# A two-block hybrid network in one launch: the first attention regrouped, the conformer stage fed further ahead

## The reference

```python
# first attention: 8 "full" heads (8 previous chunks, i.e. all keys so far, with a learned relative
# bias) and 8 heads in a window of 2 previous chunks (linear bias, sinks, 2 key/value heads)
qa, ka, va, qb, kb, vb = jnp.split(h @ w_in, cuts, axis=-1)
qa = rmsnorm(heads(qa, H_A), q_norm_a); ka = rmsnorm(heads(ka, H_A), k_norm_a)
oa = band_attention(qa, ka, heads(va, H_A), A_PREV_CHUNKS, bias_a, None)
qb = rmsnorm(heads(qb, H_B), q_norm_b); kb = rmsnorm(heads(kb, H_B_KV), k_norm_b)
ob = band_attention(qb, kb, heads(vb, H_B_KV), B_PREV_CHUNKS, bias_b, sinks)
return jnp.concatenate([oa, ob], axis=-1) @ w_out
# each head of q and k: y = x * rsqrt(mean(x*x over its 64 channels) + eps) * gain

# conformer convolution (second block)
a, gate = jnp.split(h @ w_pw1 + b_pw1, 2, axis=-1)
u = a * sigmoid(gate)
u = depthwise_conv_31_taps(u) + b_dw
u = silu(layer_norm(u, ln_g, ln_b))
return u @ w_pw2 + b_pw2
```

## Time and profile before

| | us |
|---|---|
| median of the runs (3 runs) | 3264.16 |
| the profiled execution | 3262.22 |
| its span, first to last instruction | 3260.4 |
| mean granted TensorE clock | 0.977 |
| PE busy in the span | 3083.4 (95%) |
| DVE, ACT, POOL busy | 1521.9, 1307.6, 1186.2 |
| first attention, from its first projection to its output projection | 13.4 to 290.0 |
| conformer, from its first projection to the end of the last mean matmul | 1608.4 to 1816.4 |

### The profile page before, as it was taken

One profiled execution on the slowest core, in us unless ns is written; L12 is line 12 of the kernel. 1 busy time (PEld: TensorE's weight loads), 2 busy tenths in 40 slices (PEclk: granted clock), 3 DMA queues, 4 the chain that ended last, 5 costly groups with the idle time before them and its releaser, 6 DMA issues.

```text
span 3260.4 us, 40032 instructions
## 1 busy us (share of the span) xinstructions
PE 3083.4 (95%) x13814; PEld 2393.4 (73%) x13814; DVE 1521.9 (47%) x2127; ACT 1307.6 (40%) x2069; POOL 1186.2 (36%) x511
## 2 busy tenths in 40 slices
PE   6898999998998899999988999999989999899998
PEld 4566788876675578888755777888867787788886
DVE  5542555336616735552278633333147763333222
ACT  4663444323334534443322534443233343344432
POOL 3121444442342034444432532444432253244443
PEclk8998999999998899999999999999999999999999
DMA  4121322332220022223311321222321132122332
GB/s 151 40 77 33 93 94 92 101 97 77 77 90 1 1 84 91 92 95 99 101 47 44 123 78 58 91 96 91 103 83 59 59 116 85 43 93 91 95 97 90
DMA packets 74459, 263.18 MB, mean 81 GB/s; under 512 B 8664, under 2 KB 8928, under 8 KB 74096
## 3 DMA queue, kind: packets, MB, share of 16 engines
q1 hardware_dynamic: 68400, 249.07, 24.5%
q10 hardware_dynamic: 3648, 7.46, 0.6%
q0 software_dynamic: 2304, 5.24, 0.6%
HBM read 259.59 MB, written 2.15 MB: 80 GB/s over the span
## 4 chain that ended last, share of the span: by engine, by line
PE 43%; issue 33%; POOL 14%; DVE 7%; ACT 2%; POOLq 0%; DMA 0%; ACTq 0%; DVEq 0%; SPq 0%
POOL w_lo L547 14%; PE bank L610 11%; PE bank L612 11%; PE bank L611 11%; PE bank L1109 2%; DVE bank L1785 2%; DVE bank L1877 1%; PE bank L1236 1%; PE bank L1239 1%; PE bank L1057 1%; PE bank L1058 0%; PE bank L1059 0%; PE bank L686 0%; PE bank L726 0%; PE bank L1253 0%
## 5 line engine op out<-in xcount | busy, mean ns | idle before, releaser
L547 POOL TENSOR_TENSOR w_lo<-w_raw,w_hi 128x1024 fp32r<-128x1024 f32 x475 | 1144.8, 2413 | 1901.5 <-ACT w_hi L2049 1901.5
L2049 ACT ACTIVATE w_hi<-w_raw 128x1024 fp32r<-128x1024 f32 x475 | 501.1, 1056 | 668.7 <-DMA w_raw<-w_glu_out 157.0
L610 PE MATMUL bank<-xh,w_hi 128*128 128x512 f32 x1864 | 745.3, 400 | 18.9 <-POOL w_lo L547 14.2
L611 PE MATMUL bank<-xl,w_hi 128*128 128x512 f32 x1864 | 740.0, 397 | 0.0
L612 PE MATMUL bank<-xh,w_lo 128*128 128x512 f32 x1864 | 739.8, 397 | 0.0
L610 PEld LDWEIGHTS bank<-xh,w_hi 128*128 128x128 f32 x1864 | 351.7, 189 | 114.9 <-POOL w_lo L547 21.6
L611 PEld LDWEIGHTS bank<-xl,w_hi 128*128 128x128 f32 x1864 | 351.8, 189 | 86.1 <-issue 1.7
L612 PEld LDWEIGHTS bank<-xh,w_lo 128*128 128x128 f32 x1864 | 351.8, 189 | 85.8
L1341 DVE TENSOR_TENSOR xt<-bank,xt 128x512 f32 x72 | 49.8, 692 | 504.1 <-PE bank L612 504.1
L612 PE MATMUL bank<-hh,w_lo 128*128 128x512 f32 x704 | 279.1, 396 | 0.0
L610 PE MATMUL bank<-hh,w_hi 128*128 128x512 f32 x704 | 279.1, 396 | 0.0
(11 more groups left out here) (341 smaller groups left out, 4659.2 us busy)
## 6 DMA issues: line engine op xcount, KB each, us to landing
w_raw<-w_ffn_in SPq DMA_DIRECT2D x88, 512.0 KB, 3.5
w_raw<-w_glu_in SPq DMA_DIRECT2D x88, 512.0 KB, 3.5
w_raw<-w_ffn_out SPq DMA_DIRECT2D x48, 512.0 KB, 3.5
w_raw<-w_glu_out SPq DMA_DIRECT2D x48, 512.0 KB, 3.5
w_raw<-w_ssm_in SPq DMA_DIRECT2D x41, 512.0 KB, 3.5
w_raw<-w_pw SPq DMA_DIRECT2D x24, 512.0 KB, 3.5
w_raw<-w_diff_in SPq DMA_DIRECT2D x24, 512.0 KB, 3.5
w_raw<-w_attn_in SPq DMA_DIRECT2D x18, 512.0 KB, 3.6
```

What stands on the lines that cost most here:

```text
L547: pool.tensor_tensor(w_lo[:, slot, :], w_raw[:, slot, :], w_hi[:, slot, :].bitcast(F32), ALU.subtract).then_inc(w_split, 1)
L610: pe.matmul(b, wh, hi[:, k, 0:n], start=(k == 0), stop=False)
L611: pe.matmul(b, wh, lo[:, k, 0:n], start=False, stop=False)
L2049: act.activation(w_hi[:, slot, :], w_raw[:, slot, :], ACT.Copy).then_inc(w_half, 1)
```

## The change

In the first attention: the chunk order becomes kb, qb pair 0, vb, the other qb, then (qa, ka, va) by pair. The sums of squares of a group of chunks go as rows into one bank of 32 rows (`pick`, a 128 by 32 selection); there are four groups; the root and the reciprocal (in two halves) are taken once per group on 32 rows, and a second matmul (`heads`, 32 by 128) spreads a chunk's rows to bank 5, from which DVE scales. All q, k and v of the full heads have a place of their own. The windowed heads use one set of banks only, with turn in the same step and outputs one step later; the full heads alternate between two sets as before. More units are fed per step (11 per 4 places), so that the projections end in step 12. The 128 by 128 outputs of a pair are kept until its four tiles are there, and then transposed, stored and split together. `b_pt` now lies on the memory input `m_in`, whose load moves from the kernel's start to the first ffn. In the conformer: 7 taps on PE and 24 on DVE, four buffers `c_u`, the gate stays in its PSUM bank, the projections run one pair further ahead, and ACT takes one more slab before it copies `m_hi`. The core of the diff:

```diff
-        CPE = 8
+        CPE = 7
-        VALUES = (1, 8, 11, 14, 17)
+        VALUES = (2, 8, 11, 14, 17)
+        GROUPS = ((0, 1), (3, 4, 5), (6, 7, 9, 10), (12, 13, 15, 16))
+        EARLY = (8, 8, 8, 4, 4, 4, 4)
+        SLOT0 = len(EARLY)
         def attn_fed(x):
-            return min(18 * KD, 34 + 9 * (x + 1) // 6) if x >= 0 else 34
+            if x < SLOT0:
+                return sum(EARLY[:x + 1])
+            return min(18 * KD, sum(EARLY) + 11 * (x - SLOT0 + 1) // 4)
+        def attn_events():
+            sums = {attn_at(c) + 1: c for c in NORMED}
+            roots = {attn_at(g[-1]) + 1: n for n, g in enumerate(GROUPS)}
+            shared = [(attn_at(c) + 1, c) for c in VALUES]
+            for x, n in roots.items():
+                shared += [(x + 3 + (i if n else 0), c) for i, c in enumerate(GROUPS[n])]
         def step_bank(m, half):
-            return bank[2 + 2 * (m % 2) + half]
+            return bank[2 + half + (2 if is_rel(m) and m % 2 == 0 else 0)]
+        def turn_step(m):
+            return m + 1 if is_rel(m) else m
+        def output_step(m):
+            return m + 2 if is_rel(m) else m + 1
# PE, first attention
-                    pe.matmul(bank[7][:], head_ones[:], sq[:, 0, :], start=True, stop=True).then_inc(q_sum, 1)
+                def total(c):
+                    pe.wait_ge(q_sq, n + 1)
+                    if i == 0 and g:
+                        pe.wait_ge(q_root, g)
+                    pe.matmul(bank[4][0:32, :], pick[:, 30 - 2 * i:62 - 2 * i], sq[:, 0, :], start=(i == 0),
+                              stop=(c == GROUPS[g][-1]), skip_group_check=True).then_inc(q_sum, 1)
+                def share(k):
+                    if k:
+                        pe.wait_ge(*released(k))
...
+                    pe.wait_ge(q_rec, 2 * g + 2)
+                    pe.matmul(bank[5][:], heads[:, i * P:(i + 1) * P], acc[0:32, :], start=True, stop=True).then_inc(q_bc, 1)
                 def score(m):
-                    if m >= 2:
-                        pe.wait_ge(b_copied, 2 * (m - 1))
+                    elif m == NB4 + 1:
+                        pe.wait_ge(b_copied, 2 * NB4)
+                    elif m:
+                        pe.wait_ge(b_copied, 2 * (m - 1) if is_rel(m) else 2 * m)
                 def outputs(m):
-                        pe.wait_ge(b_ol, m)
+                        pe.wait_ge(b_otok, m)
-                def turn_out(m):
-                    pe.wait_ge(b_otok, m + 1)
-                    pe.transpose(bank[6][:, P:2 * P], b_tok[:, m % 2, :], ident[:]).then_inc(b_ot, 1)
+                def turn_out(pair):
+                    pe.wait_ge(b_otok, NT * (pair + 1))
+                    if pair:
+                        pe.wait_ge(b_ol, pair)
+                    for t in range(NT):
+                        mm = pe.transpose(bank[7][:, t * P:(t + 1) * P], b_tok[:, t, :], ident[:])
+                    mm.then_inc(b_ot, 1)
# DVE, first attention
-                    dve.reciprocal(bank[7][:], bank[7][:]).then_inc(q_rec, 1)
+                def inverse(g, part):
+                    dve.wait_ge(q_root, g + 1)
+                    r = acc[0:32, part * 256:(part + 1) * 256]
+                    dve.reciprocal(r, r).then_inc(q_rec, 1)
# PE, conformer
-                project(1)
-                for p in range(KD):
-                    if p < KD - 1:
-                        project(2 * p + 2)
-                    else:
-                        feed(KD)
+                for c in range(1, 3):
+                    project(c)
+                conv(0)
+                for c in range(3, 6):
+                    project(c)
+                for p in range(1, KD):
                     conv(p)
                     if p >= 3:
                         mean(p - 3)
-                    if p < KD - 1:
-                        project(2 * p + 3)
+                    if p < KD - 2:
+                        project(2 * p + 4)
+                        project(2 * p + 5)
+                    elif p == KD - 2:
+                        feed(KD)
# DVE, conformer
-                    dve.tensor_tensor(c_g[:, p % 2, :], bank[(b0 + 1) % BANKS][:], rstd[:], ALU.mult).then_inc(bank_free, 1)
+                    dve.tensor_tensor(g[:], g[:], rstd[:], ALU.mult).then_inc(c_gate, 1)
-                    dve.scalar_tensor_tensor(c_u[:, p % 3, CONVW - 1:], c_a[:, p % 2, :], col("pw1_b", 2 * p),
-                                             c_g[:, p % 2, :], ALU.add, ALU.mult).then_inc(c_new, 1)
+                    dve.scalar_tensor_tensor(c_u[:, p % 4, CONVW - 1:], c_a[:, p % 2, :], col("pw1_b", 2 * p),
+                                             bank[(st.chunk0 + 2 * p + 1) % BANKS][:], ALU.add, ALU.mult).then_inc(bank_free, 1)
-                        if p < KD - 1 and n == (5 if p else 7):
-                            gated(p + 1)
-                        if p < KD - 1 and n == (7 if p else 9):
-                            entered(p + 1)
+                        if p == 0 and n == 2:
+                            gated(1)
+                        if p == 0 and n == 4:
+                            entered(1)
+                        if p < KD - 2 and n == 8:
+                            gated(p + 2)
+                        if p < KD - 2 and n == 9:
+                            entered(p + 2)
# ACT, conformer
                 next_slab()
                 gate(0)
                 next_slab()
+                next_slab()
                 act.wait_ge(m_landed, 16)
                 act.activation(m_hi[:], m_in[:], ACT.Copy).then_inc(m_half, 1)
                 diag(1)
+                gate(1)
+                next_slab()
                 for p in range(KD - 1):
-                    next_slab()
-                    gate(p + 1)
-                    next_slab()
-                    if p + 2 < KD:
+                    if p < KD - 2:
+                        next_slab()
+                        gate(p + 2)
+                        next_slab()
                         diag(p + 2)
# constants and the memory input
-                dve.tensor_copy(head_ones[:], cst[:, 3 * P:4 * P]).then_inc(cst_ready, 1)
+                dve.tensor_copy(pick[:], cst[:, 3 * P:3 * P + 64]).then_inc(cst_ready, 1)
+                dve.tensor_copy(heads[:].rearrange("p (a n) -> p a n", n=64),
+                                ident[0:32, 0:8].unsqueeze(2).broadcast_to([32, 8, 64])).then_inc(cst_ready, 1)
-            act.dma_start(m_in[:], A["memt"]).then_inc(m_landed, 16)
+                if s == "ffn0":
+                    act.dma_start(m_in[:], A["memt"]).then_inc(m_landed, 16)
```

More of the change, by code:

```diff
@@ L381, in attn_at @@
+        def attn_at(c):
             x = 0
-            while attn_fed(x) < min(KD * (c + 1) + extra, 18 * KD):
+            while attn_fed(x) < KD * (c + 1):
                 x += 1
-            return x + (1 if KD * (c + 1) + extra > 18 * KD else 0)
-        def step_bank(m, half):
-            return bank[2 + 2 * (m % 2) + half]
-        VALUES = (1, 8, 11, 14, 17)
-        NORMED = [c for c in range(18) if c not in VALUES]
-        UNITS = {}
+            return x
+        def attn_events():
[4 more added lines that the diff above has]
+                shared += [(x + 3 + (i if n else 0), c) for i, c in enumerate(GROUPS[n])]
+            return sums, roots, sorted(shared)
@@ L1925, in attn @@
                     for f in range(3):
[L1926 to L1936 removed]
+                        events(SLOT0 + 3 * m + f)
+                        if f == 0 and m < BM:
+                            weigh(m)
+                        for j in range(NT - 1, BM, NT):
+                            if f == 2 and output_step(j) == m:
+                                low(j // NT)
                 vt[0] += 5
@@ L2428, in square, with rooted, value, events @@
                     act.activation(sq[:, 0, :], norm_slot(c), ACT.Square).then_inc(q_sq, 1)
[L2430 to L2439 removed]
+                def rooted(g):
+                    act.wait_ge(q_sum, sum(len(chunks) for chunks in GROUPS[:g + 1]))
+                    if g:
+                        act.wait_ge(q_bc, sum(len(chunks) for chunks in GROUPS[:g]))
+                    act.activation(acc[0:32, :], bank[4][0:32, :], ACT.Sqrt, scale=1.0 / 64, bias=eps[0:32, 0:1])\
+                        .then_inc(q_root, 1)
+                def value(c):
+                    act.wait_ge(v_turned, VALUES.index(c) + 1)
+                    act.activation(b_v[:, value_slot(c), :], bank[5][:], ACT.Copy).then_inc(v_ready, 1)
+                def events(x):
+                    for c in NORMED:
+                        if attn_at(c) == x:
+                            square(c)
+                    if x in ROOTS:
+                        rooted(ROOTS[x])
+                    for at, c in SHARED:
+                        if at == x and c in VALUES:
+                            value(c)
+                    while turned[0] < 18 + LEAD and attn_fed(x) >= min(KD * (turned[0] - LEAD) + 6, 18 * KD):
+                        next_slab()
```

285 lines of the change are left out of this document (126 added, 159 removed).

## The result

The changed kernel takes 3286.8 us (median of 4 runs, 3282.2 to 3291.3) against 3265.2 in the same job: ratio 1.0074, 95% interval 1.0061 to 1.0086. I had forecast 3252, range 3232 to 3270. The profiled execution took 3282.2 (span 3280.3), 20.0 more than before's 3262.2.

The account below looks back on a forecast made before the run. PE and issue hold three quarters of the chain of waits, with engines waiting in turn. From 3262.2, 5 us lost in the attention and 17 won in the conformer give 3250, or 3252 against the median; range 3232 to 3270.

Parts of the forecast that it names:

- The conformer: Conformer stage: PE and DVE work side by side, pairs take 18 us instead of 22.2; 17 us won.
- its stop: Conformer start: PE stands 7.4 us before project(3), because the later `m_hi` copy delays POOL's `memory_lower` and subtractions.
- PE as bound of steps 0 to 12: First attention: with 104 projection units and the added norm matmuls, PE limits these steps, 118 us in total.
- the price of the added matmuls: First attention: separate norm sums and spreadings, 0.86 us each; the extra 13 cost PE 11.2 us.
- rival C: Windowed attention steps: scores wait for copies from the single bank set; 1.5 us a step gives 3276; chance 0.15.
- X + 133.0: Conformer: end of the last tap, 1797.9, counted from X = 1664.9, after the opening stop, three chunks and conv(1).
- Steps 16 to 31, without projections: Late first attention: priced from earlier projection-free steps at 82.3 us, bounds 73.3 and 91; step 31 starts at 278.3.
- rival B: First attention: clock stays down from step 14; steps 16 to 31 take 91 instead of 82, total 3261; chance 0.18.
- To step 0: First attention: step 0 starts at about 60.8 instead of 58.3, with 40 units done instead of 34.
- Steps 0 to 12: First attention: PE does 104 units plus attention and norm matmuls; step 12 starts at 173.
- Steps 12 to 15: First attention: last group's norm and bare chains take 25 us; step 16 starts at 198, effectively 196.
- The end: First attention, score 31 to output projection: two waits for `low` go, 16.4 us instead of 17.9.

Follow-up runs that it names:

- keep3: The changed kernel plus 108 extra bf16 matmuls with unused results in attention steps 16 to 33: 3263.0 us, ratio 1.0001.
- slow_feed_clock: slow_feed with the extra unused matmuls of keep3, begun in step 15: 3256.2 us, ratio 0.9976 to the kernel before.
- pool_order: keep13 with POOL's second bias table loads after the output projection's first three subtractions instead of before them: 3258.6 us, ratio 0.9976 to the kernel before.
- keep13: keep3 with the extra matmuls begun in step 13 instead of 16: 3262.6 us.
- slow_feed: The changed kernel feeding 12 projection units per five places instead of 11 per four, so projections end in step 14: 3269.6 us, ratio 1.0017.
- cheap_norm: keep13 with 9 norm sums and 9 spreadings cut to 128 of 512 columns, output not the reference's: 3245.0 us, ratio 0.993 to the kernel before.
- before_short_recip: The kernel before with DVE's 13 head norm reciprocals over 128 of 512 columns, values not the reference's: 3246.0 us, ratio 0.995.
- best_clock: m_hi_early plus the extra unused matmuls of keep3 in steps 26 to 33 of the first attention: 3235.9 us, ratio 0.9916 to the kernel before.
- m_hi_early: conf_only with the copy `m_hi` one slab earlier, in its place before the change: 3241.7 us, ratio 0.9936 to the kernel before.
- conf_only: The kernel before with only the conformer part of the change: 3246.1 us, ratio 0.995.

## Why the prediction was wrong

**Right.** The conformer: 17 forecast, 18 measured, with its stop (7.4 and 7.41) and the pairs 17.7 apart, DVE going from one to the next without a wait. PE as bound of steps 0 to 12 and the price of the added matmuls (11.2 for 13; doubling them costs 13.7). The windowed steps on one set of banks: among their scores only that of step 15 waited for `b_pt`, 0.47 us, so rival C, my slower case, named the wrong mechanism.

**Right by luck.** `entered` at 0.74: I gave it 0.7 because its operand would come from PSUM. What the traces of both kernels show is another cause, told in the last section. There are also slips in the working that move nothing: steps 0 to 15 of before feed 72 units, not 73; a pair took 22.8 us, not 22.2; and the sum to X + 133.0 has four rounds of 17.7 in it, where the text says five.

**The step that failed** is "Steps 16 to 31, without projections": 82.3 us (80.3 from step 16's own start, 198 to 278.3), upper bound 91; measured 105.1. I took its price from four steps that ran at a mean clock of 0.85 and put the upper bound for four at "about 25", 2.5 more, which is about the 2.7 that I had worked out for one of the four, step 27 (its score, bias matmuls and transposes). Four such steps took 29.2 to 30.3 here (steps 19 to 30). The rows above show why: everything that PE does in the loop is longer in every step, the outputs too, and ACT's copies and the next score wait for them. That bound was no bound. The mechanism was rival B's, at 0.18 and priced +14 with that same bound; keep3 shows 19 us in the trace and 24 in the medians. I held against it that steps 28 to 30 of before were back at full clock; their mean was 0.88 (0.74 in step 28), and in 15 such steps in a row the clock was 0.60 on the whole. By the Trainium skill ("TensorE: Matmul & The Clock Gate", What's actually happening) it is the engine's recent activity that lifts the throttle; keep3 agrees, 0.60 to 0.91 by nothing but more matmuls.

With the clock kept up by extra matmuls, the term was near: 86.1 (keep3), 82.7 (slow_feed_clock) and 76.7 (pool_order) against my 82.3 and lower bound 73.3.

**Smaller misses.** "To step 0": 64.05 instead of 60.8; the same code started step 0 at 60.71 in slow_feed_clock, at clock 0.95 instead of 0.85 in the stretch before it, so this one is the clock as well. "Steps 0 to 12": 115.9 instead of 112.2. "Steps 12 to 15": 30.0 instead of 25, at clock 0.68. I had counted their waits but not that PE, standing, falls to half clock: of the four spreadings there, 1.12 us each at full clock, two took 2.04 and 2.07. The end, on the other hand, took 11.6 instead of 16.4. With the 24.8 of the failed step (105.1 against 80.3) these are the 31.9 by which the attention came out later than the forecast 294.7. Inside the late steps lies POOL's block of DVE, 3.8 us before step 25, which I had not looked for. In before the same three subtractions stand in the late steps too (229.9 to 237.0), but the one such instruction of DVE in their time began near their end, at 236.72, and took 0.32.

**Where the 36.5 us are.** By stretches: step 16 starts 36.2 later, steps 16 to 30 take 6.7 more, the end 6.3 less. By step 16 PE has done 38 more units (26.7 us) and the 13 spreadings (11.2). The late steps should have given the units' time back, and did not. What the runs give back of the attention's end, in their profiled executions, against 290.05 before and 326.55 changed:

| | output projection starts | after the attention of before |
|---|---|---|
| keep3 | 307.77 | 17.7 |
| keep13 | 307.40 | 17.4 |
| slow_feed | 316.72 | 26.7 |
| slow_feed_clock | 292.84 | 2.8 |
| pool_order | 294.10 | 4.1 |
| cheap_norm | 293.55 | 3.5 |

Single causes, each from one comparison: 19 clock in steps 16 to 30, 11 to 14 added matmuls, 4 POOL's block, up to 3 clock in steps 12 to 15. They overlap and so are no closed account, though they come to about 36.5. The table, too, goes by one execution of each kernel: those of pool_order and slow_feed_clock are the fastest of theirs, that of keep13 the slowest.

What the shorter reciprocals gave to DVE (17.7 by before_short_recip) does not show: in steps 0 to 11 PE is full, with 99 units instead of 54. At full clock throughout, and with 90 extra matmuls in them, the late steps were 21.7 shorter (76.7 against 98.4) for 26.7 us of work less; at clock 0.60 they were 6.7 longer. So moving the units out was worth most of their price, if the clock had held. How much of the reciprocals' gain is eaten by the added matmuls and how much by the moved units no run tells apart; a kernel with the grouped norms and the old spread of projections wasn't tried, since the sums and spreadings need the banks that the full heads use.

## What to carry to other kernels

Work that fills the waits of a loop bound by latency (a loop in which engines wait for each other in turn) can also be what keeps the matrix engine's clock up. Taken away, it shortened this loop by 21.7 us at full clock (pool_order), and lengthened it by 6.7 at the clock that was granted. Price such a loop at half clock with all of its matmuls, not one group, and measure it once with extra matmuls, as keep3 does. Before crediting a faster engine, ask which engine is full in that stage afterwards; and check a change of order against the latest time that each moved transfer is needed.

## What was not expected of the hardware

Extra bf16 matmuls of 384 columns, whose results nobody uses, made the kernel faster: 108 of them 24 us in the changed kernel, and some 6 us in before's attention (best_clock against m_hi_early). They are not free: the 90 in steps 16 to 30 are 19.4 us of records in pool_order. Steps 27 to 30 took 19.8 us at full clock without them (conf_only) and 21.4 with them (pool_order, whose loop is the changed one, so the difference is not theirs alone).

The same kernel can get either clock in the same steps: steps 27 to 30 of before's attention took 22.5 us at 0.85 in before's trace and 19.8 at 1.00 in conf_only's.

A DVE instruction of 128 by 2 elements from SBUF to SBUF took 4.11 us, from 264.87 to 268.98, and POOL's three subtractions ended at 268.95; with POOL idle it took 0.17. `entered` shows the same in before. With all its operands in SBUF it took 0.75 and 0.74 us in the first two pairs, with POOL idle, and 2.13 to 2.65 the other six times, each begun during a subtraction of POOL and ended 0.54 or 0.55 us after it:
```profile
1642.15 0.74 DVE L1771 SCALAR_TENSOR_TENSOR c_u<-c_a,cols,c_g 128x512 f32<-128x512 f32 x1
...
1686.12 2.35 POOL L547 TENSOR_TENSOR w_lo<-w_raw,w_hi 128x1024 fp32r<-128x1024 f32 x1 [11.62 <-ACT w_hi L2049]
```
The one of the earlier trace rows, 1686.88 to 1689.01, is beside this subtraction, which ends at 1688.47. In the changed kernel all eight took 0.73 to 0.75, and none of them meets a subtraction. So the 1.4 to 1.9 us that these six had too much are the wait for POOL, which is gone; whether the operand in PSUM would have spared it too, no run shows. The Trainium skill ("SBUF — State Buffer", SBUF: two separate sides) says that GpSimd and some DVE instructions (a two-port mode, or two inputs in SBUF beside a GpSimd instruction that reads SBUF) share a port pair as an exclusive lock, where the loser is blocked for the other's whole instruction. Both agree with the traces, the DVE instructions ending with POOL's. But the wait of 4.11 us began in the second of three subtractions and lasted to the end of the third, so here the loser waited for more than one.
